# Key and value projection of a two-layer encoder: evictions on ScalarE, transposed tokens copied ahead of the forget gate's steps

## The chip, the cores and the metric

The kernel runs on one core of one Trainium2 chip. The metric is the device time of one execution in microseconds (us); each version is run several times and the median stands for it.

## The reference, cut to what matters

One inference step of a two-layer encoder over 1024 prompt tokens and 64 sample tokens (1088 in all) of 1024 features. Layer 0 is a differential attention with a ConvFFN and a gated input embedding. Then one projection makes keys, values and forget gates, which layer 1 (a "forgetting" attention, again with ConvFFN and embedding) shares. The change lies in that projection, at about the middle of the kernel:

```python
def shared_kv(x, kv_norm, w_kvf, b_f):
    z = rmsnorm(x, kv_norm) @ w_kvf          # 1024 -> 256 keys, 256 values, 16 gates
    k, v, f = jnp.split(z, [KV_B * DH_B, 2 * KV_B * DH_B], axis=-1)
    ...
    logf = jax.nn.log_sigmoid((f + b_f).astype(jnp.float32)).transpose(0, 2, 1)
    return k, v, logf
...
c = jnp.cumsum(logf, axis=-1)                # over cached and new tokens for the sample
s = s + cq[..., :, None] - ck[..., None, :]  # the gates enter the logits of layer 1
```

Keys, values and logf are outputs too, stored token by token.

## The kernel before, in words

Activations lie with features on the partitions and the 1088 tokens along the free axis, cut into three segments of 384, 384 and 320 tokens. Every fp32 product is made of three fp32r matmuls (high by high, high by low, low by high, lines 1161 to 1163), so a segment of one output chunk of 128 features is 24 matmuls into one PSUM bank (segment s into bank s). All engines run hand-written instruction streams in order, and counting semaphores tie them.

**TensorE** in this stage (`turn_tokens` and the loop behind it, lines 1655 to 1677) makes the gates' chunk (16 features) and then five chunks n = 0 to 4: two of keys, two of values, and the first chunk of queries. A segment may start when the same bank of the chunk before it was evicted (`kvf_kept`). After segment 0 of chunk n, `turn_tokens(n - 1)` transposes chunk n - 1, which the engine has to find fully evicted, into PSUM banks 4 and 5 in turn: three groups of up to four 128x128 blocks (line 1280), for the two key chunks a fourth group with the cached keys. Turn k may start when turn k - 2 was copied away (`t_free`), so the third group waits for the copy of the first. Only then come segments 1 and 2 of chunk n.

**VectorE** (lines 2841 to 2925) evicts the gates (line 2843) and then carries out, in one hand-written order: the steps of the log-sigmoid on a 16x1088 tile, each counted in `lf_step_v` (lines 2873 to 2900: 13 steps with a reciprocal, line 2883, and two cumulative sums, lines 2903 and 2905); `keep_kv(n)`, the three evictions of a chunk from PSUM into `kvraw` (line 2848); `keys_low(n)`, the low part of the keys (line 2853); `keep_turned(n)`, the copies of the transposed groups to `kvtok` (line 2861), and for key chunks the low part of the cached keys (line 2866); clearing `k_gates` (line 2909) once the key stores have landed (`kk_stored`); the low part of the cumulative gates (lines 2912 and 2914); two constants `pick` for the queries (line 2917) and their spreading over `q_pick` (line 2920). `keep_turned(0)` stands behind the reciprocal, `keep_turned(1)` behind two steps that follow it, and `keep_turned(2)` behind the sums.

**ScalarE** (lines 2266 to 2309) makes Exp and Ln for the gates, `keys_high(p)`: the high parts of the keys (lines 2286, 2287) and of the cached keys (line 2290), the stores `store_kv(n)` of keys and values, of the gates (lines 2297, 2298), and the high part of the cumulative gates (lines 2300, 2301). **GpSimd** (lines 893, 899 and 908) scales the next weight chunk by the norm's gain and splits it into high and low, and later splits values and pairs queries (lines 1081 to 1090). **SyncE** loads the weights, stores the split keys (lines 757 to 760) and gates, and loads them back in the form of layer 1 (line 778 and on).

Layer 1's attention begins with `scores_b(0, 0)` (line 1459), which waits for the queries, for `k_gates` and `k_twice` loaded and for `picked`.

Of the kernel before, what the change touches and what calls it, by code (L numbers as in the profile page):

```python
# [21 lines left out]
ALU = mybir.AluOpType  # L22
ACT = mybir.ActivationFunctionType
AX = mybir.AxisListType

P = 128
# [3 lines left out]
T = TP + TS  # L30
# [10 lines left out]
SEGS = [(0, 384), (384, 384), (768, 320)]  # L41
# [175 lines left out]
def program(nc, x_prompt, x_sample, p_prompt, p_sample, cache_a_k, cache_a_v, cache_b_k, cache_b_v,  # L217
# [4 lines left out]
    at = plan()  # L222
    ctx = ExitStack()
    with ctx:
# [933 lines left out]
        def _(pe):  # L1158
# [281 lines left out]
            def scores_b(n, m):  # L1440

                U, t = divmod(n, 9)
                if n:
                    pe.wait_ge(exp_done, scored(n - 1, m))
                if m == 0 and t % 3 == 0:
                    pe.wait_ge(qkv_kept, 24 + 3 * U + t // 3 + 1 if n else 27)
                    pe.wait_ge(q_paired, 3 * U + t // 3 + 1)
                if m == 0 and n == 0:
                    pe.wait_ge(picked, 1)
                if m == 0 and t == 0:  # L1450
                    pe.wait_ge(early_loaded, early_count(U))
                if m == 0 and t == 8:
                    pe.wait_ge(late_loaded, early_count(U))
                a, b = columns(t)
                width, first = width_b(n), 0 if t < 8 else TP
                for c0 in range(0, width, 512):
                    c1 = min(c0 + 512, width)
                    out = psf[:, 1024 * m + c0:1024 * m + c1]
                    pe.matmul(out, q_both[:, m, a:b], k_twice[:, first + c0:first + c1], start=True, stop=False,
                              skip_group_check=True)  # L1460
                    pe.matmul(out, q_pick[:, m, a:b], k_gates[:, first + c0:first + c1], start=False, stop=c1 < width,
                              skip_group_check=True)
                w = 128 if t < 8 else TS
                pe.matmul(psf[:, 1024 * m + width - w:1024 * m + width], ident_r[:, :], causal_r[:, P - w:P], start=False,
                          stop=True, skip_group_check=True).then_inc(s_done, 1)
# [298 lines left out]
        def _(act):  # L1764
# [508 lines left out]
            def store_kv(n):  # L2273
                act.wait_ge(t_free, KV_TURNS[n] + 3)
                for a in range(2):
                    d = slice(64 * a, 64 * a + 64)
                    dp, ds_ = ((b_k_p, b_k_s) if n < 2 else (b_v_p, b_v_s))
                    h = 2 * (n % 2) + a
                    stored = kv_stored if n < 3 else last_stored
                    act.dma_start(dp[0, h].rearrange("(b p) d -> p b d", p=P), kvtok[:, n, 0:8, d]).then_inc(stored, 16)  # L2280
                    act.dma_start(ds_[0, h], kvtok[64:P, n, 8, d]).then_inc(stored, 16)

            def keys_high(p):
                act.wait_ge(kvf_kept, 3 * p + 6)
                act.wait_ge(kk_stored, 32 * p)
                act.activation(kk_hi[:, 0:TP], kvraw[p][:, 0:TP], ACT.Copy).then_inc(kk_high, 1)
                act.activation(kk_hi[:, TP + PAST:NK], kvraw[p][:, TP:T], ACT.Copy).then_inc(kk_high, 1)
                k = KV_TURNS[p] + 3
                act.wait_ge(t_done, len(TURNED_A) + k + 1)
                act.activation(kk_hi[:, TP:TP + PAST], ps[:, 4 + k % 2, 0:PAST], ACT.Copy).then_inc(kk_high, 1)  # L2290

            keys_high(0)
            store_kv(0)
            keys_high(1)
            store_kv(1)
            act.wait_ge(lf_step_v, 10)
            act.dma_start(b_lf_p[0], fb[5][:, 0:TP]).then_inc(lf_stored, 16)
            act.dma_start(b_lf_s[0], fb[5][:, TP:T]).then_inc(lf_stored, 16)
            act.wait_ge(lf_step_v, 13)
            act.activation(c_first[:, 0:TP], fb[0][:, 0:TP], ACT.Copy, scale=-1.0).then_inc(c_high, 1)  # L2300
            act.activation(c_first[:, TP:NK], fb[3][:, 0:PAST + TS], ACT.Copy, scale=-1.0).then_inc(c_high, 1)
            store_kv(2)
            act.wait_ge(kk_stored, 64)
            for s in range(3):
                queries_high(0, s, s)
# [49 lines left out]
        def _(dve):  # L2355
            def wait_column_job(c, g, i, per_c, per_g, s):
                if s < 2:
                    dve.wait_ge(gemm_done, reg(i, per_g, g + s + 1))
                else:
                    dve.wait_ge(chunk_done, reg(i, per_c, c + 1))  # L2360
# [481 lines left out]
                wait_column_job(ck, gk, 0, 0, 0, s)  # L2842
                dve.tensor_scalar(fb[0][:, a:a + w], ps[0:16, s, 0:w], bf_col, None, ALU.add).then_inc(kvf_kept, 1)

            def keep_kv(n):
                for s, (a, w) in enumerate(SEGS):
                    wait_column_job(ck + 1 + n, gk + 2 + 2 * n, 0, 0, 0, s)
                    dve.tensor_copy(kvraw[n % 2][:, a:a + w], ps[:, s, 0:w]).then_inc(kvf_kept, 1)

            def keys_low(n):  # L2850
                dve.wait_ge(kk_high, 3 * n + 2)
                for d, k0, w in ((0, 0, TP), (TP, TP + PAST, TS)):
                    dve.tensor_tensor(kk_lo[:, k0:k0 + w], kvraw[n][:, d:d + w], kk_hi[:, k0:k0 + w].bitcast(F32),
                                      ALU.subtract).then_inc(kk_low, 1)
# [14 lines left out]
            def step(n):  # L2869
# [7 lines left out]
            dve.tensor_scalar(fb[1], fb[3], 1.0, None, ALU.subtract).then_inc(lf_step_v, 1)  # L2877
            step(3)
            dve.scalar_tensor_tensor(fb[5], fb[1], 0.0, fb[1], ALU.is_equal, ALU.add).then_inc(lf_step_v, 1)
            keep_kv(0)  # L2880
            keys_low(0)
            step(4)
            dve.reciprocal(fb[5], fb[5]).then_inc(lf_step_v, 1)
            keep_turned(0)
            keep_kv(1)
            keys_low(1)
            step(5)
            dve.tensor_tensor(fb[5], fb[2], fb[5], ALU.mult).then_inc(lf_step_v, 1)
            dve.wait_ge(lf_step_a, 2)
            step(6)  # L2890
            dve.tensor_tensor(fb[5], fb[4], fb[5], ALU.mult).then_inc(lf_step_v, 1)
            keep_turned(1)
            keep_kv(2)
            dve.scalar_tensor_tensor(fb[1], fb[1], 0.0, fb[2], ALU.is_equal, ALU.mult).then_inc(lf_step_v, 1)
            step(8)
            dve.tensor_tensor(fb[5], fb[5], fb[1], ALU.add).then_inc(lf_step_v, 1)
            step(9)
# [6 lines left out]
                                   ALU.add).then_inc(lf_step_v, 1)  # L2904
            dve.tensor_tensor_scan(fb[3][:, 0:PAST + TS], one[0:16].broadcast_to([16, PAST + TS]), lcat, 0.0, ALU.mult,
                                   ALU.add).then_inc(lf_step_v, 1)
            keep_turned(2)
            dve.wait_ge(kk_stored, 64)
            dve.memset(k_gates[64:P, :].bitcast(F32), 0.0).then_inc(gates_cleared, 1)
            dve.wait_ge(c_high, 2)  # L2910
            dve.wait_ge(lf_stored, 32)
            dve.scalar_tensor_tensor(c_second[:, 0:TP], fb[0][:, 0:TP], -1.0, c_first[:, 0:TP].bitcast(F32), ALU.mult,
                                     ALU.subtract).then_inc(c_low, 1)
            dve.scalar_tensor_tensor(c_second[:, TP:NK], fb[3][:, 0:PAST + TS], -1.0, c_first[:, TP:NK].bitcast(F32),
                                     ALU.mult, ALU.subtract).then_inc(c_low, 1)
            keep_kv(3)
            dve.tensor_tensor(pick[:, 0:2], ident[:, 64:66], ident[:, 66:68], ALU.add).then_inc(pick_made, 1)
            dve.wait_ge(pick_made, 1)
            for m in range(2):
                p = dve.tensor_copy(q_pick[64:P, m, :], pick[64:P, m:m + 1].broadcast_to([64, T]))  # L2920
            p.then_inc(picked, 1)
            keep_turned(3)
            for s in range(3):
                queries_low(0, s, s)
# [100 lines left out]
```

## Time and profile before

| | us |
|---|---|
| median of three runs | 3167.29 (3164.74 to 3167.58) |
| the profiled execution, its own time | 3164.45 |
| its span | 3162.7 |
| TensorE busy | 2975.1 (94%) |
| VectorE, GpSimd, ScalarE busy | 2118.5, 1535.0, 1325.1 |
| mean granted TensorE clock | 0.982 of full speed |

The span is the time from the first to the last instruction, and 1.75 us of the profiled execution's time lie around it. The stage that is changed runs from about 1650 to 1745 us of the span. In the rows, PE is TensorE, DVE VectorE, ACT ScalarE, POOL GpSimd and SP SyncE; `t` is any SBUF tile, `ps` the PSUM.

### The profile page before, as it was taken

The page shows a single profiled execution, that of the slowest core. Times are in us where ns is not written, and L with a number is a line of the kernel's source. Part 1 is how long each engine was busy: PE and PEld are TensorE (multiplying, and loading weights), DVE is VectorE, ACT ScalarE, POOL GpSimd, SP SyncE. Part 2 cuts the span into 40 slices and gives each one's busy share as a digit, 9 for nine tenths or more (in the row PEclk, how much of TensorE's full clock was granted, in tenths as well). Part 3 has the DMA queues.
Part 4 walks back from the last instruction along what each step waited for, and adds up shares of the span by engine and source line. Part 5 has one row for each costly group of instructions (what it writes and reads, how often), then busy time and mean ns, then how long its engine had stood idle before and what let it go on. Part 6 is the DMA issues. An engine that isn't in the chain of part 4 may idle for free.

```text
span 3162.7 us, 47548 instructions
## 1 busy us (share of the span) xinstructions
PE 2975.1 (94%) x18469; PEld 2865.9 (91%) x18469; DVE 2118.5 (67%) x3217; ACT 1325.1 (42%) x2678; POOL 1535.0 (49%) x975
## 2 busy tenths in 40 slices
PE   7999999898999999999987999999889999999998
PEld 6888888797999999999977888889889999999997
DVE  5666666429888887335776677762888888733475
ACT  5555555314444443113340666651444444411243
POOL 2222222235888884122334777763478888512231
PEclk8999999899999999999998999999999999999999
DMA  5232222311222224211114121131122222421111
GB/s 116 63 79 71 63 70 91 109 41 51 76 72 75 78 71 156 103 61 56 40 25 123 36 60 52 50 131 41 39 78 78 72 76 79 159 101 61 56 41 64
DMA packets 282191, 234.24 MB, mean 74 GB/s; under 512 B 29860, under 2 KB 264052, under 8 KB 281972
## 3 DMA queue, kind: packets, MB, share of 16 engines
q1 hardware_dynamic: 267160, 217.29, 23.0%
q10 hardware_dynamic: 14812, 13.97, 1.4%
q8 instruction: 145, 2.38, 0.3%
q14 instruction: 74, 0.61, 0.1%
HBM read 168.63 MB, written 62.58 MB: 73 GB/s over the span
## 4 chain that ended last, share of the span: by engine, by line
PE 74%; DVE 14%; ACT 6%; issue 3%; DMA 1%; POOL 1%; ACTq 0%; SPq 0%; DVEq 0%; POOLq 0%
PE ps L1161 21%; PE ps L1163 21%; PE ps L1162 20%; PE ps L1344 2%; ACT t L1927 2%; PE ps L1479 2%; PE ps L1297 2%; PE ps L1280 2%; PE ps L1364 1%; DVE t L2563 1%; DVE t L2398 1%; DVE t L2486 1%; DVE t L2413 1%; DVE ps L2478 1%; ACT t L1983 1%
## 5 line engine op out<-in xcount | busy, mean ns | idle before, releaser
L1161 PE MATMUL ps<-t,t 128*128 128x384 f32 (+1 forms) x4760 | 1595.2, 335 | 70.3 <-ACT t L2099 14.3
L1163 PE MATMUL ps<-t,t 128*128 128x384 f32 (+1 forms) x4760 | 1564.0, 329 | 0.0
L1162 PE MATMUL ps<-t,t 128*128 128x384 f32 (+1 forms) x4760 | 1562.6, 328 | 0.0
L1161 PEld LDWEIGHTS ps<-t,t 128*128 128x128 f32 x4760 | 902.1, 190 | 104.4 <-issue 43.0
L1162 PEld LDWEIGHTS ps<-t,t 128*128 128x128 f32 x4760 | 902.8, 190 | 1.0 <-issue 0.2
L1163 PEld LDWEIGHTS ps<-t,t 128*128 128x128 f32 x4760 | 901.3, 189 | 0.0
L943 POOL TENSOR_TENSOR t<-t,t 128x512 fp32r<-128x512 f32 x280 | 468.1, 1690 | 43.9 <-ACT t L2049 34.8
L899 POOL TENSOR_TENSOR t<-t,t 128x1024 fp32r<-128x1024 f32 x101 | 250.8, 2483 | 482.3 <-ACT t L1814 478.9
L2764 DVE TENSOR_TENSOR t<-t,ps 128x384 f32<-128x384 f32 (+1 forms) x240 | 126.3, 531 | 276.6 <-PE ps L1163 276.6
L2698 DVE SCALAR_TENSOR_TENSOR t<-t,t,t 128x1090 f32<-128x1090 f32 x88 | 191.3, 2173 | 93.0 <-ACT t L2045 91.6
L2049 ACT ACTIVATE t<-t 128x512 fp32r<-128x512 f32 x320 | 193.7, 625 | 126.8 <-POOL t L951 48.4
L893 POOL TENSOR_TENSOR t<-t,t 128x1024 fp32r<-128x1024 f32 x51 | 106.0, 2078 | 262.0 <-PE ps L1163 261.4
L1814 ACT ACTIVATE t<-t 128x1024 fp32r<-128x1024 f32 x50 | 53.0, 1059 | 381.8 <-PE ps L1163 381.8
L1114 POOL TENSOR_TENSOR t<-t,t 128x128 f32<-128x128 f32 (+5 forms) x144 | 162.3, 1148 | 103.8 <-DVE t L2941 102.2
L2045 ACT ACTIVATE t<-t,t 128x1090 f32<-128x1090 f32 x88 | 115.0, 1307 | 229.1 <-DVE t L2683 229.1
L2700 DVE SCALAR_TENSOR_TENSOR t<-t,t,t 128x1090 f32<-128x1090 f32 x88 | 188.8, 2145 | 3.1
L2563 DVE TENSOR_TENSOR t<-ps,t 128x512 fp32r<-128x512 f32 (+1 forms) x184 | 115.6, 632 | 68.6 <-ACT t L1983 66.1
L1927 ACT ACTIVATE t<-ps,t 128x128 f32<-128x128 f32 (+5 forms) x144 | 105.9, 739 | 93.7 <-DVE t L2486 93.7
L1983 ACT ACTIVATE t<-ps 128x512 fp32r<-128x512 f32 (+1 forms) x184 | 101.5, 551 | 93.9 <-PE ps L1280 90.5
L1012 POOL TENSOR_TENSOR t<-t,t 128x384 fp32r<-128x384 f32 (+1 forms) x24 | 23.2, 968 | 226.1 <-ACT t L1951 226.1
L1280 PE MATMUL ps<-t,t 128*128 128x128 f32 x700 | 109.6, 275 | 24.6 <-DVE t L2861 20.6
L1479 PE MATMUL ps<-t,t 128*128 128x256 f32 (+1 forms) x656 | 118.8, 298 | 13.8 <-DVE t L2589 6.3
(192 smaller groups left out, 4078.8 us busy)
## 6 DMA issues: line engine op xcount, KB each, us to landing
t<-in_w_ffn_in SPq DMA_DIRECT2D x160, 256.0 KB, 2.9
ff_dram<-t SPq DMA_DIRECT2D x44, 544.0 KB
t<-ff_dram SPq DMA_DIRECT2D x44, 544.0 KB, 6.7
t<-in_w_ffn_out SPq DMA_DIRECT2D x44, 512.0 KB, 3.4
t<-in_w_qkv_a SPq DMA_DIRECT2D x24, 512.0 KB, 4.0
t<-in_w_ple_gate SPq DMA_DIRECT2D x16, 512.0 KB, 3.8
out<-t SPq DMA_DIRECT2D x32, 192.0 KB, 2.1
t<-in_w_o_a SPq DMA_DIRECT2D x8, 512.0 KB, 4.1
```

The source lines that it names most:

```text
L899: pool.tensor_tensor(w_lo[slot][:, :], w_raw[slot][:, :], w_hi[slot][:, :].bitcast(F32), ALU.subtract).then_inc(w_split, 1)
L943: pool.tensor_tensor(lo, raw, hi.bitcast(F32), ALU.subtract).then_inc(blk_split, 1)
L1114: pool.tensor_tensor(probs, probs, rz[:, c + m:c + m + 1].broadcast_to([P, w]), ALU.mult).then_inc(scaled, 1)
L1161: pe.matmul(out, a_hi, b_hi, start=start, stop=False, skip_group_check=True)
L1162: pe.matmul(out, a_hi, b_lo, start=False, stop=False, skip_group_check=True)
L1163: return pe.matmul(out, a_lo, b_hi, start=False, stop=stop, skip_group_check=True)
L1280: m = pe.transpose(ps[:, bank, 128 * b:128 * b + rows], src, ident[0:rows, 0:rows])
L1479: mm = pe.matmul(ps[:, 6, 0:256], v_both[r:P, vi, :], part[r:P, k % 2, 256 * b:256 * b + 256], start=g == 0 and b == 0 and part is bT_hi, ...
L1927: act.activation(p_a[n % 2][:, m, 0:w], psf[:, 1024 * m:1024 * m + w], ACT.Exp, bias=negmax[:, col:col + 1], accum_out=zsum[:, col:col + 1 ...
L2049: act.activation(S[name][0], S[name][2], ACT.Copy).then_inc(blk_high, 1)
L2698: dve.scalar_tensor_tensor(dst, ub[:, 1:T + 3], col(44), dst, ALU.mult, ALU.add).then_inc(conv_step, 1)
L2700: dve.scalar_tensor_tensor(dst, ub[:, 0:T + 2], col(0), dst, ALU.mult, ALU.add).then_inc(conv_step, 1)
```

## The change

VectorE no longer evicts the key and value chunks: `keep_kv` moves to ScalarE, which evicts segment by segment (with waits for `t_free` and `kk_low` from the third chunk on, since `kvraw` has two buffers that it may not overwrite), placed between its other work. `keys_high` is cut in two: the cached keys' high part becomes `cached_high`, and the eviction of the next chunk's segment 0 stands between the two. The spreading of the query constants moves to ScalarE as well, so `picked` counts to 2. On VectorE the copies of the transposed tokens come earlier or later against the gate's steps: `pick` is made before the reciprocal; `keys_low(0)` behind it; the three steps of lines 2888, 2891 and 2894 together behind `keep_turned(0)`, and then `keys_low(1)` and `keep_turned(1)`; `keep_turned(2)` goes from ahead of the clearing of `k_gates` to behind it.

```diff
@@ TensorE, scores_b
-                    pe.wait_ge(picked, 1)
+                    pe.wait_ge(picked, 2)
@@ ScalarE
+            def cached_high(p):
                 k = KV_TURNS[p] + 3
                 act.wait_ge(t_done, len(TURNED_A) + k + 1)
                 act.activation(kk_hi[:, TP:TP + PAST], ps[:, 4 + k % 2, 0:PAST], ACT.Copy).then_inc(kk_high, 1)
 
+            ck, gk = at["K"]
+
+            def keep_kv(n, segments):
+                for s in segments:
+                    a, w = SEGS[s]
+                    if n >= 2 and s == 0:
+                        act.wait_ge(t_free, KV_TURNS[n - 2] + 3)
+                        act.wait_ge(kk_low, 2 * (n - 1))
+                    wait_column_job(ck + 1 + n, gk + 2 + 2 * n, 0, 0, 0, s)
+                    act.activation(kvraw[n % 2][:, a:a + w], ps[:, s, 0:w], ACT.Copy).then_inc(kvf_kept, 1)
+
+            act.wait_ge(kvf_kept, 3)
+            keep_kv(0, (0, 1, 2))
             keys_high(0)
+            keep_kv(1, (0,))
+            cached_high(0)
             store_kv(0)
+            keep_kv(1, (1, 2))
             keys_high(1)
+            keep_kv(2, (0,))
+            cached_high(1)
             store_kv(1)
             act.wait_ge(lf_step_v, 10)
             act.dma_start(b_lf_p[0], fb[5][:, 0:TP]).then_inc(lf_stored, 16)
             act.dma_start(b_lf_s[0], fb[5][:, TP:T]).then_inc(lf_stored, 16)
+            keep_kv(2, (1, 2))
             act.wait_ge(lf_step_v, 13)
             act.activation(c_first[:, 0:TP], fb[0][:, 0:TP], ACT.Copy, scale=-1.0).then_inc(c_high, 1)
             act.activation(c_first[:, TP:NK], fb[3][:, 0:PAST + TS], ACT.Copy, scale=-1.0).then_inc(c_high, 1)
+            keep_kv(3, (0,))
             store_kv(2)
+            act.wait_ge(pick_made, 1)
+            for m in range(2):
+                act.activation(q_pick[64:P, m, :], pick[64:P, m:m + 1].broadcast_to([64, T]), ACT.Copy).then_inc(picked, 1)
+            keep_kv(3, (1, 2))
             act.wait_ge(kk_stored, 64)
@@ VectorE
-            def keep_kv(n):
-                for s, (a, w) in enumerate(SEGS):
-                    wait_column_job(ck + 1 + n, gk + 2 + 2 * n, 0, 0, 0, s)
-                    dve.tensor_copy(kvraw[n % 2][:, a:a + w], ps[:, s, 0:w]).then_inc(kvf_kept, 1)
...
             dve.scalar_tensor_tensor(fb[5], fb[1], 0.0, fb[1], ALU.is_equal, ALU.add).then_inc(lf_step_v, 1)
-            keep_kv(0)
-            keys_low(0)
+            dve.tensor_tensor(pick[:, 0:2], ident[:, 64:66], ident[:, 66:68], ALU.add).then_inc(pick_made, 1)
             step(4)
             dve.reciprocal(fb[5], fb[5]).then_inc(lf_step_v, 1)
+            keys_low(0)
             keep_turned(0)
-            keep_kv(1)
-            keys_low(1)
             step(5)
             dve.tensor_tensor(fb[5], fb[2], fb[5], ALU.mult).then_inc(lf_step_v, 1)
             dve.wait_ge(lf_step_a, 2)
             step(6)
             dve.tensor_tensor(fb[5], fb[4], fb[5], ALU.mult).then_inc(lf_step_v, 1)
+            dve.scalar_tensor_tensor(fb[1], fb[1], 0.0, fb[2], ALU.is_equal, ALU.mult).then_inc(lf_step_v, 1)
+            keys_low(1)
             keep_turned(1)
-            keep_kv(2)
-            dve.scalar_tensor_tensor(fb[1], fb[1], 0.0, fb[2], ALU.is_equal, ALU.mult).then_inc(lf_step_v, 1)
             step(8)
...
-            keep_turned(2)
             dve.wait_ge(kk_stored, 64)
             dve.memset(k_gates[64:P, :].bitcast(F32), 0.0).then_inc(gates_cleared, 1)
+            keep_turned(2)
             dve.wait_ge(c_high, 2)
             dve.wait_ge(lf_stored, 32)
...
-            keep_kv(3)
-            dve.tensor_tensor(pick[:, 0:2], ident[:, 64:66], ident[:, 66:68], ALU.add).then_inc(pick_made, 1)
-            dve.wait_ge(pick_made, 1)
-            for m in range(2):
-                p = dve.tensor_copy(q_pick[64:P, m, :], pick[64:P, m:m + 1].broadcast_to([64, T]))
-            p.then_inc(picked, 1)
             keep_turned(3)
```

## Rows read from the trace of the kernel before

**Rows 1.** The page's first part: busy time of each engine
```profile
PE 2975.1 (94%) x18469; PEld 2865.9 (91%) x18469; DVE 2118.5 (67%) x3217; ACT 1325.1 (42%) x2678; POOL 1535.0 (49%) x975
```

**Rows 2.** The waits, 1650 to 1750 us: us in total, times, longest
```profile
PE ps L1280 <- DVE t L2861: 20.6, 6, 8.9
```

**Rows 3.** Timeline of TensorE: start, us, engine, line, operation, idle before
```profile
1675.88 0.47 PE L1280 MATMUL ps<-t,t 128*128 128x128 f32 x1 [7.18 <-DVE t L2861]
...
1690.11 1.03 PE L1280 MATMUL ps<-t,t 128*128 128x128 f32 x8
...
1694.28 0.33 PE L1280 MATMUL ps<-t,t 128*128 128x128 f32 x1 [3.14 <-DVE t L2861]
...
1708.89 1.03 PE L1280 MATMUL ps<-t,t 128*128 128x128 f32 x8
...
1718.78 0.47 PE L1280 MATMUL ps<-t,t 128*128 128x128 f32 x1 [8.85 <-DVE t L2861]
...
1734.88 0.33 PE L1280 MATMUL ps<-t,t 128*128 128x128 f32 x1 [0.87 <-DVE t L2861]
...
1744.90 0.33 PE L1459 MATMUL ps<-t,t 128*128 128x128 f32 x1 [2.00 <-DVE t L2554]
```

**Rows 4.** Timeline of VectorE, columns as before
```profile
1659.03 0.54 DVE L2848 COPY t<-ps 128x384 f32<-128x384 f32 x1
...
1665.27 3.16 DVE L2853 TENSOR_TENSOR t<-t,t 128x1024 fp32r<-128x1024 f32 x2 [1.27 <-ACT t L2287]
1668.35 6.93 DVE L2883 RECIPROCAL t<-t 16x1088 f32<-16x1088 f32 x1
1675.21 1.47 DVE L2861 COPY t<-ps 128x512 f32<-128x512 f32 x3
...
1693.55 1.47 DVE L2861 COPY t<-ps 128x512 f32<-128x512 f32 x3
...
1708.08 2.87 DVE L2896 TENSOR_TENSOR t<-t,t 16x1088 f32<-16x1088 f32 x1
...
1714.61 2.28 DVE L2903 TENSOR_TENSOR_SCAN t<-t,t 16x1024 f32<-16x1024 f32 x1
...
1718.07 1.51 DVE L2861 COPY t<-ps 128x512 f32<-128x512 f32 x3
1719.97 1.39 DVE L2909 MEMSET t<- 64x1600 f32 x1 [0.39 <-issue]
...
1729.39 1.62 DVE L2917 TENSOR_TENSOR t<-t 128x2 f32<-128x2 f32 x1
...
1734.14 1.49 DVE L2861 COPY t<-ps 128x512 f32<-128x512 f32 x3
```

**Rows 5.** Busy time by stretch: PE, PEld, DVE, ACT, POOL, then clock, DMA
```profile
1677.00:1680.00 3.00, 3.00 (x15) 3.00 (x14) 1.16 (x2) 0.60 (x1) 0.00 (x0) 0.64 0.50 120
...
1696.00:1700.00 4.00, 4.00 (x16) 4.00 (x15) 1.16 (x2) 0.23 (x1) 1.84 (x1) 0.57 0.87 261
...
1719.00:1724.00 5.00, 5.00 (x18) 5.00 (x18) 4.32 (x6) 0.81 (x2) 0.00 (x0) 0.55 0.50 111
...
1735.00:1739.00 4.00, 4.00 (x24) 4.00 (x25) 1.74 (x4) 0.00 (x0) 3.73 (x3) 1.00 0.91 219
```

**Rows 6.** Timeline of GpSimd: splitting of two weight chunks
```profile
1665.59 2.75 POOL L893 TENSOR_TENSOR t<-t,t 128x1024 fp32r<-128x1024 f32 x1
1668.43 2.35 POOL L899 TENSOR_TENSOR t<-t,t 128x1024 fp32r<-128x1024 f32 x1
...
1706.99 2.82 POOL L893 TENSOR_TENSOR t<-t,t 128x1024 fp32r<-128x1024 f32 x1
```

**Rows 7.** ScalarE's groups by form: busy, mean ns of one, idle before
```profile
L1777 ACT ACTIVATE t<-t 128x1088 f32<-128x1088 f32 x42 | 46.8, 1114 | 173.3 <-DVE t L2625 140.8 <-DVE t L2372 29.4 <-DVE t L2824 3.0
...
L1951 ACT ACTIVATE t<-ps 128x384 f32<-128x384 f32 x16 | 7.8, 485 | 0.0
```

**Rows 8.** Line 760, the store of the keys' low part
```profile
DMA to landing us min/median/max: 7.1/7.3/7.4
```

## The prediction

> **What bounds the kernel now.** I read the page first: TensorE is busy for 94% of the span [rows 1], so time is won only where TensorE idles or runs slowly. Then the waits between 1650 and 1750 us: one cause holds almost all of TensorE's idle time there, the transposes of line 1280 that wait for VectorE's copies of line 2861, 20.6 us in six waits [rows 2]. The timeline of TensorE puts them in place: 7.18 us ahead of 1675.88, 3.14 ahead of 1694.28, 8.85 ahead of 1718.78, 0.87 ahead of 1734.88 [rows 3]; the two left out are short ones directly behind the first two. Each is the third group of `turn_tokens`, which needs the first group's bank. VectorE's timeline says why the copy was late: it stood behind the reciprocal (1668.35, 6.93 us), behind a chain of gate steps, and behind the last steps and both sums (from 1708.08 to 1718.07) [rows 4]. Last the stretches: behind the three long waits the granted clock is 0.64, 0.57 and 0.55, near the lower level (1.2 GHz), behind the short one it is 1.00 (2.4 GHz) [rows 5]. The counts in rows 5 price that: 24 matmuls fit into the 4 us at full clock, 15 into 3 us, 16 into 4 us and 18 into 5 us behind the waits, so 3, 8 and 12 matmuls were lost, at 0.167 us each 0.5, 1.3 and 2.0 us, 3.8 in all. The stage thus holds 20.6 + 3.8 = 24.4 us that no matmul needs.
>
> **The change part by part.** I rebuild the stage with the durations of this execution and carry the lead of each point over its old time.
>
> *First turn.* The twelve evictions leave VectorE (about 0.54 us each, 6.5 us together [rows 4]). More counts that they no longer make it wait in order: it is free at 1659.03, where the first eviction stood. The addition for `pick` took 1.62 us on 2 columns [rows 4]; it was held by GpSimd. The rows show this alternation: the keys' low parts took 3.16 us [rows 4] while GpSimd split weights, and GpSimd's line 893 stretched to 2.75 and 2.82 [rows 6]. I take 1.9 us for `pick` (1659.0 to 1661.0) as an instruction of line 893 is under way then; the reciprocal runs to 1667.9. `keys_low(0)` now stands behind it and needs up to 3.5 us between GpSimd's instructions: 1671.4. So the first copy starts 3.8 us before its 1675.21, and the wait of 7.18 falls to 3.4.
>
> Here a row can be read two ways. The reciprocal overlaps line 899 of GpSimd (1668.43, 2.35 us [rows 6]) from its start: either it lasts 6.93 us by itself, or 6.93 - 2.35 = 4.6 us after waiting for it. In the second case it ends at 1667.9 as well, because it waits for line 899 now too, but pushes GpSimd's next chunk against `keys_low(0)`, and the lead is 2.2. I take the first, as line 899 shows no stretching at 2.35 us, and keep 2.2 as an end.
> The Trainium skill (SBUF — State Buffer, section Who interferes with whom) says that a VectorE instruction with at most one SBUF input, outside the two-port modes, does not contend with GpSimd. By that rule the reciprocal isn't held and the lead is 3.8; by the other reading the sum below would be 1.6 us smaller. No row before isolates it.
>
> *Second turn.* All that feeds it moves by 3.8: the stores of the first keys, the high parts of the second, `keys_low(1)`. The three gate steps now between `keep_turned(0)` and `keys_low(1)` take about 1.2 us each without GpSimd, and fill a hole in which VectorE only waited for evictions. TensorE reaches the turn at 1690.11 - 3.8 = 1686.3, its first group is done 0.5 later, and VectorE is ready at 1685.7. So the copy starts at 1686.85 instead of 1693.55 [rows 3, 4]: lead 6.7. What stays of the wait is like the fourth (0.87), behind which the clock was 1.00, so the 1.3 us of slow matmuls go: lead 8.0. A lower clock staying is the other end, 6.7.
>
> *Third turn.* TensorE reaches it at 1708.89 - 8.0 = 1700.9, group one done at 1701.4. VectorE, free from the second at 1690.2, makes step 8 behind GpSimd's current instruction (up to 1692.3), steps 9 and 10 to 1694.7, the sums (3.46 us from 1714.61 to 1718.07 [rows 4]) to 1698.4, or to 1700.3 if the next weight chunk, split from 1696.9 on, gets in between, as with line 2896 (2.87 us against some 1.2 [rows 4]). Then the clearing, new ahead of the copies: it waits for the key stores, issued at 1690.2 and landed 7.3 us later [rows 8] at 1697.9, so already there, and costs 0.39 + 1.39 us [rows 4], or 2 more if GpSimd holds it. The copy starts between 1701.4 and 1704.1; I take 1703.0 instead of 1718.07, lead 15.1. Of the 2.0 us of slow clock I give back half (the wait left is 1 to 3 us, between the 0.87 that cost nothing and the 3.14 that did): 16.1.
>
> *Fourth turn.* VectorE has neither the constants' spreading nor the last evictions ahead, so it is no longer 0.6 us late (1734.14 against a first group done at about 1733.5): 16.7.
>
> *ScalarE.* An eviction costs 0.485 us there [rows 7], about 5.6 in all, and the two spreadings 1.11 each by the nearest form [rows 7], half the partitions; 1.5 each if the broadcast reads worse. The engine idles for most of the stage, so what counts is order. Segments 1 and 2 of the third chunk stand behind step 10 (forecast 1694.7) and two DMA issues (0.8 us): evicted at 1696 and 1697.4, needed at 1700.9. Those of the fourth stand behind step 13 (1698.4 to 1700.3), `store_kv(2)`, whose four issues take 2.3 us, and the spreadings: ready at about 1709, needed at 1715. Slack 3.5 and 6 us, cost nothing; when that cover is gone each us late costs TensorE one.
>
> *What is late next.* Behind the stage the scores wait for gates, constants and paired queries. The last eviction of queries comes 16.7 us earlier. The reload of the gates runs behind line 2914, which leads by about 15, and the values' load behind it; GpSimd splits these first and pairs the queries next. The pairing has about 3 us to spare, of which 1.5 are used. No loss in the forecast, 1 to 2 us at the edge. SyncE's and ScalarE's DMAs are the same ones, all moved with their data.
>
> The sum is a lead of 16.7, with half a us of the first clock loss perhaps returned: 17 us. Ends: 1.6 less for the reciprocal, 1.3 and 1.0 less for the clock, 1.1 less for the copy, 2 less at the end give 10; 1.6 and 1.0 more for the third turn and 0.5 for the clock give 20. Against the profiled execution, 3164.45 - 17 = 3147.5; its time stands 2.8 below the median of the three, by which the same is 3150.3. I forecast 3148.8, between the two.
>
> **The rivals.** (a) *The third wait stays in part.* The sums and the clearing interleave with GpSimd, or the key stores land late, and the slow clock stays. For it: every two-input step of rows 4 that met GpSimd took twice its time. Against: the forecast already has most of it. Lead 9 to 14, 3155.
>
> (b) *The gain is absorbed ahead of layer 1.* The reload of gates and values and GpSimd's pairing of queries get later than TensorE. For: their lead is smaller than TensorE's. Against: before, the scores waited for line 2554 of VectorE alone (2.00 us at 1744.90 [rows 3]). Lead 6 to 10, 3159.
>
> (c) *Slower: ScalarE's evictions are held by the gate steps.* Place: `keep_kv(2, (1, 2))` behind step 10. If the steps kept their old times (step 10 at 1714.3, the sums at 1718.1), the third turn could begin only at 1714.3 + 0.8 + 1.0 = 1716.1, and the copy, now behind the clearing, at 1720.0 + 1.4 = 1721.4 instead of 1718.07: 3.3 us slower. It decides by more than 0.2% from a copy at about 1724.5, that is 6.3 us late, which step 13 at 1721 would give: 3174. Against: 15 us of waiting for evictions leave VectorE's stream ahead of step 10.
>
> (d) *The change doesn't do what it says*: the waits were not VectorE's order but a transfer. Rows 2 name the copies in every case, so I give it almost nothing: 3166.
>
> **How the numbers follow.** Forecast (3144.5 to 3153) 0.62; (a) 0.20; (b) 0.08; (c) 0.03, and (d) 0.03; 0.04 remain for a lead over 20 through a clock that never falls. A change of 0.2% (6.3 us) is about what a measurement of this kernel tells from none. Faster: 0.62 + 0.20 + 0.04 and most of (b), 0.92; within: 0.05; slower: 0.03. The range holds the forecast and (a): 3144.5 to 3157.
>
> **What would show it.** In the new profile TensorE's waits on line 2861 should be about 3.4, 0.9, 1 to 3 and 0.3 us; the reciprocal should start at about 1661 and the third turn's copy at 1703; the clock behind the second turn should be 1.00; scores should begin at about 1728. A wait of TensorE for a ScalarE eviction, or a copy later than 1706, would prove the forecast wrong, and so would a scores' start later than the queries' last low part.

## The result, and the profile after

The changed kernel's first six runs have a median of 3142.25 us (3140.15 to 3149.68) against 3166.94 for the kernel before; the ratio is 0.9927, interval 0.9914 to 0.994. That is 24.7 us less where 18 were forecast, and 2.3 us under the stated range. Two further sets of five runs gave 3147.39 (ratio 0.9933, 0.992 to 0.9947) and 3145.11 (0.9934, 0.992 to 0.9948). All 16 runs together have a median of 3145.1, the 41 of the kernel before shown with them 3166.35: 21.2 us less.

The profiled execution (3143.03 us, span 3141.2, mean clock 0.984) shows where it went. I count the stage from the start of VectorE's first gate eviction to TensorE's first score matmul: before from 1650.65 to 1744.90 [rows 3], 94.25 us; after from 1648.32 to 1722.79, 74.47 us, so 19.8 less. The gate eviction itself came 2.3 us earlier, at a point that the change doesn't touch.

TensorE's waits, 1650 to 1750 us, and its timeline (start, length, engine, line, operation, idle before):

```profile
PE ps L1280 <- DVE t L2882: 5.8, 6, 2.5
```

```profile
1668.95 0.33 PE L1280 MATMUL ps<-t,t 128*128 128x128 f32 x1 [2.54 <-DVE t L2882]
...
1682.01 1.03 PE L1280 MATMUL ps<-t,t 128*128 128x128 f32 x8
...
1683.39 0.33 PE L1280 MATMUL ps<-t,t 128*128 128x128 f32 x1 [0.35 <-DVE t L2882]
...
1696.43 1.03 PE L1280 MATMUL ps<-t,t 128*128 128x128 f32 x8
...
1699.33 0.33 PE L1280 MATMUL ps<-t,t 128*128 128x128 f32 x1 [1.86 <-DVE t L2882]
...
1712.77 0.33 PE L1280 MATMUL ps<-t,t 128*128 128x128 f32 x1 [0.35 <-DVE t L2882]
...
1722.79 0.42 PE L1459 MATMUL ps<-t,t 128*128 128x128 f32 x1 [1.99 <-DVE t L2580]
```

These answer to [rows 2, 3]: line 2861 is now 2882 and 2554 is 2580. The four waits fell from 7.18, 3.14, 8.85 and 0.87 to 2.54, 0.35, 1.86 and 0.35, their sum with the short ones from 20.6 to 5.8 us. The wait ahead of the first score is the same 2.0 us. The clock by stretch answers to [rows 5] (columns as there):

```profile
1670.00:1674.00 4.00, 4.00 (x26) 4.00 (x25) 2.96 (x3) 0.60 (x1) 0.65 (x1) 1.00 0.69 218
1684.00:1688.00 4.00, 3.92 (x24) 3.96 (x25) 2.72 (x4) 0.60 (x1) 3.84 (x3) 1.00 0.59 154
1699.00:1703.00 4.00, 3.67 (x22) 3.67 (x23) 3.66 (x5) 0.48 (x1) 1.92 (x1) 1.00 0.47 103
```

Behind all three turns it is 1.00 where before it was 0.64, 0.57 and 0.55. The stage as a whole, before and after:

```profile
1650.00:1745.00 95.00, 72.30 (x412) 69.97 (x411) 59.82 (x60) 11.79 (x18) 44.78 (x20) 0.89 0.47 120
1648.00:1723.00 75.00, 67.19 (x411) 65.04 (x412) 49.01 (x45) 19.00 (x31) 43.67 (x19) 1.00 0.57 152
```

The time came from two places: 14.8 us of waits, and some 5 us of matmuls at the lower clock (TensorE was busy for 72.3 us with 412 matmuls before and for 67.2 us with 411 after).

VectorE's timeline answers to [rows 4]:

```profile
1656.69 1.84 DVE L2901 TENSOR_TENSOR t<-t 128x2 f32<-128x2 f32 x1
1658.46 6.93 DVE L2903 RECIPROCAL t<-t 16x1088 f32<-16x1088 f32 x1
1665.32 2.98 DVE L2874 TENSOR_TENSOR t<-t,t 128x1024 fp32r<-128x1024 f32 x2
1668.22 1.47 DVE L2882 COPY t<-ps 128x512 f32<-128x512 f32 x3
...
1691.59 2.28 DVE L2922 TENSOR_TENSOR_SCAN t<-t,t 16x1024 f32<-16x1024 f32 x1
1693.80 2.98 DVE L2924 TENSOR_TENSOR_SCAN t<-t,t 16x576 f32<-16x576 f32 x1
1697.16 1.39 DVE L2927 MEMSET t<- 64x1600 f32 x1 [0.39 <-issue]
1698.59 1.49 DVE L2882 COPY t<-ps 128x512 f32<-128x512 f32 x3
```

The third turn's copies start 19.5 us earlier than in rows 4, 17.2 counted from the stage's start. ScalarE evicts in 0.44 to 0.49 us each, and the two spreadings of the query constants took 2.11 us together:

```profile
1692.27 0.82 ACT L2303 ACTIVATE t<-ps 128x384 f32<-128x384 f32 x2 [6.94 <-DVE t L2919]
...
1702.52 2.11 ACT L2327 ACTIVATE t<-t 64x1088 fp32r<-64x1088 f32 x2 [3.71 <-issue]
1704.64 0.49 ACT L2303 ACTIVATE t<-ps 128x384 f32<-128x384 f32 x1
```

The third chunk's evictions did wait 6.94 us behind step 10, as forecast, and cost nothing: they ended at 1693.1, and the transposes that need them began at 1696.43.

### The profile page after: what moved, and what is told of

Its sections match the earlier page's. It is cut to its first block, busy times and chain, and to the rows that moved or that the text cites. A ratio compares the mean times of both kernels' runs of the same rounds, so it can differ in the third digit from the quotient of the medians.

```text
span 3141.2 us, 47551 instructions
## 1 busy us (share of the span) xinstructions
PE 2969.8 (95%) x18469; PEld 2859.4 (91%) x18469; DVE 2105.6 (67%) x3203; ACT 1329.8 (42%) x2692; POOL 1542.2 (49%) x975
## 4 chain that ended last, share of the span: by engine, by line
PE 74%; DVE 15%; ACT 6%; issue 3%; POOL 1%; DMA 1%; ACTq 0%; SPq 0%; DVEq 0%; POOLq 0%
PE ps L1161 21%; PE ps L1163 21%; PE ps L1162 21%; PE ps L1344 2%; ACT t L1927 2%; PE ps L1479 2%; PE ps L1297 2%; PE ps L1280 2%; PE ps L1364 1%; DVE t L2589 1%; DVE t L2512 1%; DVE t L2424 1%; DVE ps L2504 1%; DVE t L2439 1%; ACT t L1983 1%
## 5 line engine op out<-in xcount | busy, mean ns | idle before, releaser
L951 POOL TENSOR_TENSOR t<-t,t 128x512 f32<-128x512 f32 x40 | 78.6, 1965 | 90.8 <-issue 41.2
```

## The experiments

**The changed kernel again.** No edit.

> The changed kernel once more, to part what the change does from what one execution or one set of runs does. The stage is counted from the start of VectorE's first gate eviction to TensorE's first score matmul: 94.25 us before (1650.65 to 1744.90), 74.47 after (1648.32 to 1722.79), 19.8 less. Theory A (the gain is the stage's alone): stage within 1 us of 74.5, and the median difference to the kernel before 18 to 22 us, nearer to the profiles' stage than to the 24.7 of the first set. Theory B (there is a further gain outside the stage): difference again 24 or more with a stage of 74.5.

Measured: 3147.39 us against 3166.04, 18.7 less; stage 1655.8 to 1730.6, 74.8 us. A third set was taken with the last group of runs:

> The changed kernel a third time, beside the others on the same chip. Theory A (the 24.7 us between the first medians hold some 20 us of the stage and a scatter of several us that comes from the clock outside of it): stage (first gate eviction to first score) 74.3 to 75.1 us, median 18 to 23 us under the kernel before, and single executions again spread over 6 us or more. Theory B: under 18 or over 24 with the same stage, which would name a part outside the stage that the change moves.

Measured: 3145.11 against 3166.79, 21.7 less; stage 1649.97 to 1725.59, 75.6 us, its far edge missed by half a us. The stage repeats within 1.2 us while single executions run from 3140.15 to 3150.05. Theory A holds: against the one profile of the kernel before, the stage carries 18.6 to 19.8 us, and of the first set's 24.7 some 5 us lie outside it, which the other sets don't repeat. In the first profile the gates' eviction came 2.3 us earlier than before, in the second 5.1 us later, both ahead of anything changed: of two executions of one program, 6.1 us apart in span, the longer was 7.4 us late before the stage began. It had the mean clock 0.982 instead of 0.984.

The clock behind the first turn's wait, in the first profile 1.00, fell in the other two. The first line is the second profile's (wait 2.58 us), the second the third's (2.59 us):

```profile
1676.40:1680.40 4.00, 3.75 (x15) 3.49 (x16) 2.37 (x4) 0.60 (x1) 1.73 (x1) 0.59 0.30 68
1670.70:1674.70 4.00, 3.78 (x13) 3.52 (x14) 2.36 (x4) 0.60 (x1) 1.69 (x1) 0.50 0.31 68
```

TensorE reached the second turn 1.2 and 2.6 us later in them, counted from the stage's start, but the stage is only 0.35 and 1.1 us longer: the third turn's wait shrank from 1.86 us to 1.00 and 0.35, as VectorE's copy came at 50.3, 50.6 and 51.4 us of the stage.

**Evictions alone.** VectorE's order as before, evictions on ScalarE, the constants back on VectorE.

```diff
 VectorE, against the kernel before:
-            keep_kv(0)
             keys_low(0)
             step(4)
             dve.reciprocal(fb[5], fb[5]).then_inc(lf_step_v, 1)
             keep_turned(0)
-            keep_kv(1)
...
 ScalarE: as in the changed kernel, without the spreading of pick
```

> Evictions on ScalarE alone, VectorE's order and the constants as before. Theory A (order of the copies and evictions are two halves, and only the third turn was late because of evictions): waits of TensorE at the first and second turn stay near 7.2 and 3.1 us, that at the third falls from 8.85 to under 1, with the slow clock behind it gone: stage 82 to 85 us, 9 to 12 less than before. Theory B (the evictions were what held VectorE everywhere): all waits fall and the stage comes to 76 or less. Theory C (ScalarE's evictions behind the gate's steps cost TensorE time): a wait of TensorE ends with line 2303 or the stage stays over 90.

Measured: 3156.52 us (ratio 0.9967, 0.9954 to 0.9981), stage 1651.02 to 1737.65, 86.6: 7.6 us less, under the 9 to 12 expected. TensorE's timeline:

```profile
1676.26 0.48 PE L1280 MATMUL ps<-t,t 128*128 128x128 f32 x1 [7.19 <-DVE t L2879]
...
1697.16 0.47 PE L1280 MATMUL ps<-t,t 128*128 128x128 f32 x1 [4.49 <-DVE t L2879]
...
1713.72 0.33 PE L1280 MATMUL ps<-t,t 128*128 128x128 f32 x1 [0.35 <-DVE t L2879]
```

The first wait stays and the third goes, as theory A said. The second did not stay but grew from 3.14 to 4.49, and 15 matmuls ran in the 4 us behind it, where 24 fit. VectorE stood waiting for the second keys' high part there:

```profile
DVE t L2871 <- ACT t L2287: 16.1, 2, 10.0
```

So an eviction moved to an idle engine wins the third turn alone, where VectorE used its time to run ahead; at the other two the copies still stand behind the same work.

**Order alone.** Evictions and constants on VectorE, each `keep_kv` ahead of the keys' low part or behind the turned copies.

```diff
+            dve.tensor_tensor(pick[:, 0:2], ident[:, 64:66], ident[:, 66:68], ALU.add).then_inc(pick_made, 1)
+            step(4)
+            dve.reciprocal(fb[5], fb[5]).then_inc(lf_step_v, 1)
             keep_kv(0)
             keys_low(0)
-            step(4)
-            dve.reciprocal(fb[5], fb[5]).then_inc(lf_step_v, 1)
             keep_turned(0)
             keep_kv(1)
-            keys_low(1)
...
```

> VectorE's new order alone, with evictions and constants on VectorE. Theory A: the reciprocal ahead of the first evictions makes TensorE wait some 5 us for bank 0, the first turn's wait falls to under 2, the second's to about 1, the third's stays at 6 to 8, as steps 8 to 10 still stand behind the third chunk's evictions: stage 85 to 90 us. Theory B (order is the whole effect): stage under 78. With the run before it the parts should add to about the 19.8 of the whole if they are independent.

Measured: 3161.14 us (0.9979, 0.997 to 0.9989), stage 1650.4 to 1740.43, 90.0: 4.2 us less. TensorE's waits:

```profile
PE ps L1280 <- DVE t L2861: 12.4, 6, 9.5
PE ps L1161 <- DVE t L2848: 4.8, 1, 4.8
```

The 4.8 us for bank 0 are there, with the clock at 0.50 behind them, the first two turns are nearly free, and the third is 9.5, worse than before and than expected: TensorE reaches it sooner while steps 8 to 10 still stand behind the third chunk's evictions. The two halves give 7.6 + 4.2 = 11.8 of 19.8 in the stage; in the medians of this group, 9.5 + 4.9 = 14.4 of 18.7 us. They are not independent: the early reciprocal costs nothing only because no eviction stands behind it any more, and ScalarE's evictions pay at all turns only with the copies placed ahead.

**A pause.** One more reciprocal, into a tile that nothing reads.

```diff
+            for _ in range(1):
+                dve.reciprocal(rstd[0:16, 0:T], one[0:16].broadcast_to([16, T]))
             keep_turned(2)
```

> The changed kernel with a pause: VectorE makes one more reciprocal of 16x1088 (6.93 us, into a tile that nothing reads) ahead of the third turn's copies. It measures what a long wait of TensorE costs beyond its own length. The third wait should be 8.0 to 9.0 us instead of 1.0 to 1.9. Theory A (the slow clock follows the wait): the granted clock behind it falls to near 0.5 for several us and the stage grows by 8.5 to 9.5 us, 83 to 84 us. Theory B (the slow stretches come by themselves): clock near 1.00 behind it, stage 81 to 81.5.

Measured: 3154.23 us; stage 1653.9 to 1735.9, 82.0. The wait came to 5.60 us, not 8 to 9: up to the second turn's copy the execution is the second profile's within 0.1 us, but from there to the clearing VectorE was 2.2 us faster, so of the 6.93 us only 4.7 reached the copy. The second sum took 1.32 us here and 2.98 there, line 2915 took 2.44 and 3.12.

```profile
1709.91 0.47 PE L1280 MATMUL ps<-t,t 128*128 128x128 f32 x1 [5.60 <-DVE t L2882]
```

```profile
1710.00:1716.00 6.00, 6.00 (x21) 6.00 (x22) 2.50 (x4) 2.10 (x2) 0.00 (x0) 0.54 0.69 127
1716.00:1720.00 4.00, 4.00 (x29) 4.00 (x27) 0.00 (x0) 0.49 (x1) 0.00 (x0) 1.00 0.39 102
```

The size was off, the mechanism is clear: 21 matmuls in 6 us at 0.54 where 36 fit, so 2.5 us were lost beside the wait itself. The stage grew by 7.1 us over the second profile's 74.8, 4.6 of wait and 2.5 of clock. This is the test of the clock term: the lower clock (1.2 GHz) follows the wait, at a place where the changed kernel had none.

**Three moves.** Three orders that still keep TensorE waiting in the changed kernel.

```diff
 VectorE
-            keys_low(0)
             keep_turned(0)          # the three copies alone
+            keys_low(0)
+            cached_low(0)           # the cached keys' low part, split from keep_turned
...
+            keep_turned(2)
             dve.wait_ge(kk_stored, 64)
             dve.memset(k_gates[64:P, :].bitcast(F32), 0.0).then_inc(gates_cleared, 1)
-            keep_turned(2)
 ScalarE
-            for s in range(3):
-                queries_high(0, s, s)
-            store_kv(3)
+            queries_high(0, 0, 0)
+            store_kv(3)
+            for s in (1, 2):
+                queries_high(0, s, s)
```

> The changed kernel with three more moves: the first turn's copies ahead of the keys' low part, the third turn's copies ahead of the clearing of the gates' tile, and the last value stores issued behind the queries' segment 0 instead of behind all three. Theory A (TensorE's waits are the order of VectorE and ScalarE alone): first wait from 2.54 to about 0.35, third from 1.86 to about 0.35, and the first exponentials of layer 1 start 1 us earlier against the first score: stage 70.5 to 71.5, whole kernel 4 to 5 us under the changed one. Theory B (GpSimd's weight splitting or a DMA takes the waits' place): stage 73 or more.

Measured: 3143.58 us (0.9926, 0.9912 to 0.9939), stage 1654.35 to 1726.66, 72.3: between the two theories, and 3.8 us under the changed kernel's median of the same group. All turns wait 0.35 us, as theory A says, but a new wait stands ahead of the score. TensorE and GpSimd:

```profile
1726.66 0.44 PE L1459 MATMUL ps<-t,t 128*128 128x128 f32 x1 [3.26 <-issue]
```

```profile
1721.56 1.57 POOL L1081 TENSOR_TENSOR t<-t,t 128x832 fp32r<-128x832 f32 x1 [5.12 <-DMA t<-in_cache_b_v]
1723.21 1.94 POOL L1083 TENSOR_TENSOR t<-t,t 128x832 fp32r<-128x832 f32 x1
1725.11 4.09 POOL L1089 TENSOR_TENSOR t<-t,t 64x768 fp32r<-64x768 f32 x3
```

The first of the pairings of line 1089 (1.46 us each) ends at 1726.57, and the score starts: it waits for GpSimd, which waited for the values.

**Four moves.** The pairing of the first queries' first segment ahead of the values.

```diff
 GpSimd
+            pair_queries(0, 0)
             split_values(0)
-            for s in range(3):
+            for s in (1, 2):
                 pair_queries(0, s)
```

> The kernel of three moves, with GpSimd's pairing of the first queries ahead of its splitting of the values. Theory A (in the run of three moves the first score no longer waited for VectorE but for the pairing, which stood behind values that landed late): the wait ahead of the first score falls from 3.26 to about 2.0 us and ends with VectorE's line of the queries' low part, the stage (first gate eviction to first score) falls from 72.3 to 71.0 us, and the lead over the changed kernel grows from under 1 us at layer 1's third tile to 4. Theory B (the reload of the gates and keys was what the score waited for): stage stays at 72 or more.

Measured: 3139.35 us (0.9913, 0.9899 to 0.9926), stage 1650.6 to 1721.66, 71.1:

```profile
1721.66 0.33 PE L1460 MATMUL ps<-t,t 128*128 128x128 f32 x1 [1.99 <-DVE t L2582]
```

The wait and the stage are theory A's within 0.1 us. Counted to layer 1's first value product the path is 84.9 us, against 88.6, 88.9 and 89.8 in the three profiles of the changed kernel and 87.7 with three moves. The median of its five runs (3136.58 to 3140.53) lies 5.8 us under that of the changed kernel's sixteen, which are of other groups of runs; against the kernel before in the same group the ratios are 0.9913 here and 0.9927 to 0.9934 there.

**The clearing behind the copies, alone**, the second of the three moves.

> Of the three moves only that of the third turn's copies ahead of the clearing of the gates' tile. Theory A: third wait from 1.0 to 1.9 down to 0.35, stage 73 to 73.8 instead of 74.5 to 74.8. Theory B (the copies wait for the transposes, not for the clearing): no change.

Measured: 3142.0 us in one execution; third wait 0.35 as expected, but stage 1648.6 to 1723.71, 75.1, no better. The wait ahead of the first score grew to 2.88 us: the clearing came at 51.9 us of the stage instead of 48.5 to 49.2, and behind it GpSimd's pairing. Its first part ended at 1723.61, 0.1 us before the score; the view names line 2580, which was done at 1722.77. What the turn won was handed back 25 us on. That the move pays together with the pairing's is what four moves suggest; the two alone were not run.

**The constants' spreading back on VectorE.**

```diff
 VectorE
+            dve.wait_ge(pick_made, 1)
+            for m in range(2):
+                p = dve.tensor_copy(q_pick[64:P, m, :], pick[64:P, m:m + 1].broadcast_to([64, T]))
+            p.then_inc(picked, 1)
             keep_turned(3)
```

> The changed kernel with the spreading of the query constants back on VectorE, ahead of the fourth turn's copies. VectorE idled 9.36 us there, so by theory A (the constants' move is worth nothing by itself) the fourth wait stays at 0.35 and the stage at 74.5 to 74.8. Theory B (it freed the fourth turn): fourth wait 1 us or more, stage over 75.3.

Measured: 3144.65 us in one execution; fourth wait 0.35, so the constants' move is worth nothing at its place. The stage was 72.3 and not 74.5, though, with a first wait of 0.63 instead of 2.5. VectorE and GpSimd at the step ahead of the reciprocal, here and in the changed kernel:

```profile
1658.55 1.28 DVE L2897 SCALAR_TENSOR_TENSOR t<-t 16x1088 f32<-16x1088 f32 x1
...
1658.63 2.96 POOL L908 TENSOR_TENSOR t<-t,t 128x1024 f32<-128x1024 f32 x1 [30.23 <-DMA t<-in_w_kvf_b]
```

```profile
1653.64 1.97 POOL L908 TENSOR_TENSOR t<-t,t 128x1024 f32<-128x1024 f32 x1 [29.91 <-DMA t<-in_w_kvf_b]
...
1653.89 2.87 DVE L2900 SCALAR_TENSOR_TENSOR t<-t 16x1088 f32<-16x1088 f32 x1
```

It is a race for the port that the two engines share: whichever comes first makes the other wait, and it is decided by the landing of a weight chunk within 0.3 us. In all 14 profiles VectorE's step comes 5.57 or 5.58 us behind the stage's start. In nine, line 908 began at 5.28 to 5.49 us and VectorE's step took 2.87 to 2.95 us; in five (this run, the pairing alone, three, four and five moves) it began at 5.66 to 5.85 us, took 2.76 to 2.96 us itself, and VectorE's step 1.28. Where VectorE was first, the reciprocal started 1.6 us sooner. All three profiles of the changed kernel had GpSimd first; whether an edit shifts the landing or chance does isn't shown.

**The pairing alone.**

> The changed kernel with only the pairing of the first queries ahead of the values' splitting on GpSimd. Theory A (the pairing is late only when the stage is shorter than in the changed kernel): nothing changes, first wait ahead of the score 2.0, stage 74.3 to 75.1. Theory B (the pairing is already late there): stage 73.5 or less.

Measured: 3142.47 us in one execution, stage 1650.2 to 1722.31, 72.1. By the expectation's number that would be theory B. But GpSimd's line 908 took 2.95 us there and the first wait was 0.60: VectorE had won the race, as in the run before, which reached 72.3 without this edit. The wait ahead of the score was the same 1.99. So the pairing by itself changed nothing, and the run is read against spread_back, not against the changed kernel.

**The first copies ahead of the keys' low part, alone.**

> Of the moves only that of the first turn's copies ahead of the keys' low part. Theory A (the keys' low part and GpSimd between its two instructions keep the first copy waiting): first wait from 2.5 to 0.35, no slow clock behind it, and 2 us less to the first value product, 86.3 to 86.9, unless the first score comes to wait for something else. It also tells about GpSimd's second weight chunk: its line 893 took 4.9 to 5.0 us in the changed kernel, where the keys' low part was ready and queued behind the reciprocal. If the queued instruction held the port, line 893 takes 1.9 here, since copies out of PSUM stand behind the reciprocal; if the reciprocal held it, it stays over 3.

Measured: 3140.58 us in one execution, stage 1648.7 to 1720.41, 71.7, first wait 0.35, 85.8 us to the first value product, half a us better than expected. GpSimd had won the race here (2.89 for VectorE's step), so the move does away with what the race costs at the first turn. GpSimd's second weight chunk, here and in the changed kernel:

```profile
1661.65 1.90 POOL L908 TENSOR_TENSOR t<-t,t 128x1024 f32<-128x1024 f32 x1 [0.25 <-PE ps L1163]
1663.63 1.90 POOL L893 TENSOR_TENSOR t<-t,t 128x1024 fp32r<-128x1024 f32 x1
```

```profile
1661.31 1.90 POOL L908 TENSOR_TENSOR t<-t,t 128x1024 f32<-128x1024 f32 x1 [0.30 <-PE ps L1163]
1663.29 4.93 POOL L893 TENSOR_TENSOR t<-t,t 128x1024 fp32r<-128x1024 f32 x1
```

In both the reciprocal runs on until after 1665. With copies out of PSUM queued behind it, line 893 takes 1.90 us; with the keys' low part queued and ready, 4.93. So the reciprocal does not hold the port, and the instruction behind it does, before it starts. With the constants' spreading back, line 893 began only 0.50 us before the end of the reciprocal (1668.46), and its delay is that much shorter:

```profile
1667.96 3.33 POOL L893 TENSOR_TENSOR t<-t,t 128x1024 fp32r<-128x1024 f32 x1
```

**A fifth move.** An exponential of one column behind the first queries' high parts, to have the table loaded.

```diff
+            act.activation(small[:, 30:31], zero, ACT.Exp)
```

> The kernel of four moves with a fifth: one exponential of a single column, whose result nothing reads, behind the high parts of the first queries on ScalarE. Measured from the first gate eviction to layer 1's first value product (line 1479; 108.4 us before, 88.6 and 88.9 in the two profiles of the changed kernel, 84.9 with four moves). Theory A (the table load of 1.28 us stands between the first score and the first exponential and fits into ScalarE's idle time ahead of it): no table load in front of the first exponentials, 83.5 to 83.9 us, median 1 to 1.5 us under that of four moves. Theory B (something else is as late): 84.5 or more.

Measured: 3141.34 us (0.9919, 0.9906 to 0.9933), 85.0 us to the first value product, against 84.9 with four moves. The load did go into the idle time (from 1720.24), and the first exponential started 1.0 us after the first score's matmul instead of 2.3. Nothing came of it: theory B. What is as late in this profile is TensorE itself. The first scores are followed by nine filling matmuls of the queries, which ran without a gap until the second scores, most of them in this stretch at the lower clock (15 matmuls in 3 us, where 18 fit):

```profile
1723.00:1726.00 3.00, 3.00 (x15) 3.00 (x14) 0.28 (x1) 0.21 (x2) 0.75 (x1) 0.63 0.41 92
```

The profile of four moves has the lower clock at the same place (0.50 from 1722 to 1724). Where the clock was full there, TensorE did wait for the exponentials ahead of the second scores, as in the third profile of the changed kernel:

```profile
1729.65 0.38 PE L1459 MATMUL ps<-t,t 128*128 128x256 f32 x1 [1.53 <-ACT t L1989]
```

What the fifth move would give in such an execution isn't shown; the medians show no gain.

## Why the prediction was right or wrong, point by point

*What bounds the kernel*: right. The waits on line 2861 were the whole matter, and they fell.

*First turn*: mis-sized. The lead of the first copy was put at 3.8 us and is 4.7 counted from the stage's start (4.6 in the other two profiles), the wait left 2.5 instead of 3.4. The reciprocal starts where it was expected within 0.2 us and lasts 6.93 us. Of the two readings the first was right: it lasts 6.93 us in every profile, also where line 893 and not 899 ran at its start (the constants' spreading back on VectorE), and line 893 ran beside it in 1.90 us in the experiment with the copies first. The rule of the Trainium skill (SBUF — State Buffer, Who interferes with whom), that a VectorE instruction with at most one SBUF input, outside the two-port modes, doesn't contend, agrees with that. `keys_low(0)` took 2.98 us, not 3.5, as its first instruction held the port when the reciprocal ended.

*The third turn and the clock*: the steps that failed. The leads over the kernel before, in us and counted from the stage's start, in the forecast and in the three profiles of the changed kernel:

| | forecast | first | second | third |
|---|---|---|---|---|
| first copy | 3.8 | 4.7 | 4.6 | 4.6 |
| second turn begins | 3.8 | 5.8 | 4.6 | 3.2 |
| its copy | 6.7 | 8.6 | 7.4 | 5.9 |
| third turn begins | 8.0 | 10.1 | 8.9 | 7.5 |
| its copy | 15.1 | 17.2 | 16.8 | 16.0 |
| fourth turn begins | 16.1 | 19.3 | 18.9 | 18.1 |
| first score | 16.7 | 19.8 | 19.4 | 18.6 |

Two steps explain the difference. The first is the lead of 15.1 at the third copy. I put that copy at 1703.0, 52.4 us of the stage, behind the sums and the clearing; it came at 50.3, 50.6 and 51.4. The second is the clock behind the third wait. I gave back half of its 2.0 us, since a wait of 1 to 3 us was to be left; it came back whole, 2.1 us, in all three. In the first profile these are 2.1 and 1.1 us of the 3.1 between 16.7 and 19.8.

The clock behind the first wait was mis-sized too, and there the first profile had luck. I priced its loss at 0.5 us from a stretch that began 1.1 us behind the wait, and so left out the transposes at the lower clock (0.47 us for the first and 1.09 for four, against 0.33 and 0.63 at the full clock). I left it standing, with half a us as "perhaps". In the first profile all of it came back, 1.1 us; in the second nothing did, and in the third the stretch cost 1.4 us more than before. Most of that was made up at the third copy, which in the first two profiles stood behind VectorE's own steps and not behind TensorE.

*Second to fourth turn*: the terms of the waits were right at the second turn (2.9 forecast, 2.8 measured), and at the third in the first profile (7.1 and 7.0; 7.9 and 8.5 in the others). The clock behind the second wait gave back 1.5 or 1.6 where 1.3 was forecast. The waits left are 0.35 to 0.40 at the second turn (0.9 was named), 1.86, 1.00 and 0.35 at the third, where 1 to 3 was said, and 0.35 at the fourth, as forecast.

*ScalarE*: right; the evictions behind steps 10 and 13 had 3.3 us of slack at the third turn, and rival (c), the slower one, did not occur. Rival (a) did not either.

*What is late next*: right as a place, for a shorter stage. Rival (b), GpSimd's pairing, did not bind in the changed kernel, though with little to spare (its first part, begun at 1720.76 and 1.46 us long, ended 0.6 us before the score), and did at once with three moves (3.26 us) and with the clearing moved (2.88 us).

*From the stage to the median*: wrong. The range was built from the terms of the stage, with no room for the scatter of the rest. The changed kernel's executions spread over 10 us; the median of six lay 2.9 us under that of sixteen, and that of sixteen, 3145.1, lies just inside the range. Against it the forecast of 3148.8 is 3.7 us too high. The lead of 17 us, taken from the median of the 41 runs before, would give 3149.35, 4.2 too high: 1.6 to 2.8 of that the stage has in its profiles, the rest lies outside it or is scatter, and no run parts the two. Why executions differ by up to 10 us is not shown; in the pair that was compared above the difference arose ahead of the stage.

## What to carry to other kernels

Moving evictions to an idle engine and moving what TensorE waits for ahead of long steps are one change: here they give 7.6 and 4.2 us alone and 19.8 together. When a wait of TensorE goes, count the slow matmuls behind it as well. At the turns of this stage they came back wholly where the wait fell under 2 us; behind 2.54 to 2.59 us the clock stayed full in one execution of five. A gain that TensorE makes ahead of a turn is lost again where the copy stands behind VectorE's own steps. A win in the middle of a stage is worth only what the next latest chain leaves of it; follow the same lead to the next stage's first instruction before adding it up.

## What the runs showed of the hardware that was not expected

- A two-input VectorE instruction that is ready and queued behind a reciprocal kept GpSimd off the shared port: line 893 took 4.93 to 5.04 us in five executions and 3.32 and 3.33 in two where it began nearer to the end of the reciprocal, instead of 1.89 or 1.90 in the five with copies out of PSUM queued there. In all seven its time is what was left of the reciprocal, 0.93 us of the queued instruction, and its own 1.90.
- The same port is given by order of arrival within 0.3 us, and which engine is first moved the first wait between 0.6 us (two executions) and 2.54 to 2.59 us (five), and the stage between 72.1 or 72.3 and 74.5 or more, among programs that are the same up to there.
- Waits of 2.54 to 2.59 us at the same place were followed by a granted clock of 1.00 in one execution and of 0.50 to 0.59 over the next 4 us in four; waits of 4.49 and 5.60 us by 0.50 in both; those of the second to fourth turn, up to 1.86 us in the three profiles, by 1.00.
- The wait ahead of the first score, 1.99 us, was followed by 4 us at 0.57 in the first and second profile of the changed kernel and at 1.00 in the third. From the score to the first value product all three took 14.1 us: at full clock TensorE waited for the exponentials there instead.
